# One stage for experts, overflow and the last norm of a hybrid decoder layer

## Chip, core and metric

The kernel is one program on one core of a Trainium2 chip. The metric is the device time of one execution in microseconds (us), and a kernel's time is the median of its runs. Everything is computed in float32.

## What is computed

One layer of a decoder trunk on 1024 real and 16 meta tokens of width 1024: a combined input projection, latent attention, a gated linear recurrence, a gated merge with an output projection, then a mixture of 64 experts, and a last RMS norm. The change touches only what follows the routing. The reference there, cut down:

```python
def hier_moe(xf, w_group, b_group, w_route, b_route, w1, w3, w2):
    g_logits = (xf @ w_group + b_group).astype(jnp.float32)
    ...
    gate = (p_sel * jax.nn.softmax(top_val, axis=-1)).astype(xf.dtype)
    expert = g_sel[:, None] * EXPERTS_PER_GROUP + top_idx        # two experts per token
    ...
    def expert_block(args):
        tok, e = args
        xb = x_pad[tok]
        hdn = jax.nn.silu(xb @ w1[e]) * (xb @ w3[e])
        return hdn @ w2[e]
    ...
# in reference():
        h = h + merged @ w_out[l]
        u = rmsnorm(h, ffn_norm[l])
        h = h + hier_moe(u.reshape(B * L, D), ...)
    return rmsnorm(h, final_norm)[:, N_META:]
```

Each of 1024 tokens goes to two of 64 experts. An expert has 3 MB of weights: w1 and w3 (1024 x 256 each) and w2 (256 x 1024).

## The kernel before

The program is a row of stages. Each is a block in which five engines have their own instruction streams and meet only at semaphores; at its end all engines drain, a barrier follows, the stage's semaphores are cleared, and a second barrier follows. Four stages matter here.

`phase_output` computes the residual `h` and the normed `u2`, stores both to memory, and routes: a table says which tokens each expert gets, 64 slots to an expert in the first pass. While it runs it also loads the weights of experts 0 to 2 (`AHEAD = 3`).

`phase_experts` works through the 64 experts in order. All engines run the same loop `each_expert`, whose iteration `e` holds work for several neighbouring experts:

- SyncE (SP) loads the weights of expert `e + 3` into buffer `(e + 3) % 4`, w1 and w3 (`load_up`) once the up product of expert `e - 1` has been made, w2 (`load_down`) once its down product has.
- GpSimd (POOL) gathers the 64 token rows of expert `e + 3` into `m_x` by an indirect DMA (L1908), and scatters the result of expert `e - 2` from `m_y` to `y_moe` by another (L1915), in this order.
- TensorE (PE) makes the up product of `e` (L1992, 32 matmuls), turns the rows of `e + 1` (L2001), makes the down product of `e - 1` (L2010), and turns `m_hid` of `e` (L2016).
- ScalarE (ACT) makes the sigmoid of `e`, copies the turned rows of `e + 1`, and copies the down product of `e - 1`, scaled, into `m_y`.
- VectorE (DVE) copies the row numbers for the gather of `e + 3` (`m_src_row`, L1962), those for the scatter of `e` (`m_dst_row`, L1967), makes `m_prod` and `m_hid` of `e` (L1969, L1971), and copies the turned `m_hid` (`m_hT`, L1973).

There are `NBUF = 4` buffers of the weights, of `m_x`, of `m_y` and of both kinds of row numbers. A buffer of row numbers for the scatter is used again when the scatter that read it has landed, so VectorE waits in iteration `e` for the scatter of `e - 4`:

```python
                if inside(e):
                    if inside(e, -NBUF):
                        dve.wait_ge(y_out[b], 16 * n)
                        settle(dve, g)
                    dve.tensor_copy(dst_row[b][:, :], rows[:, 0, bass.ds(e, 1)]).then_inc(dst_ok, 1)
                    dve.wait_ge(sig_ok, e + 1)
```

`phase_overflow` does the experts that have more than 64 tokens; each engine reads the largest count and branches (L2045). In the profile nothing of its loop runs. `phase_final` walks 8 tiles of 128 tokens: SP loads `z_h` (512 KB) and the two expert results of each token `z_y` (1 MB) four tiles ahead; VectorE adds both (L2227), ScalarE squares, sums and takes the root (L2214, L2216), VectorE inverts (L2230) and multiplies (L2233), and GpSimd issues the store (L2204). `z_y` can't be loaded before the last scatter has landed, and the whole of `phase_final` starts behind it.

Of the kernel before, what the change touches and what calls it, by code (L numbers as in the profile page):

```python
# [48 lines left out]
NBUF = 4  # L49
AHEAD = 3  # L50
SKIP = 4096.0
# [1771 lines left out]

def inside(e, d=0):

    return not isinstance(e, int) or 0 <= e + d < EXPERTS


def each_expert(eng, body):

    for e in range(-3, NBUF):
        body(e, e // NBUF, e % NBUF)
    with eng.Fori(1, EXPERTS // NBUF - 1) as n:
        for b in range(NBUF):
            body(NBUF * n + b, n, b)
    for e in range(EXPERTS - NBUF, EXPERTS + 3):
        body(e, e // NBUF, e % NBUF)


def turn(n, b, d):  # L1840


    return n + (b + d) // NBUF, (b + d) % NBUF


def phase_experts(nc, g):

    HALF = DE // 2
    with ExitStack() as ph:
# [7 lines left out]
        y = [sb(f"m_y{b}", [CAP, D]) for b in range(NBUF)]  # L1862
# [7 lines left out]
        y_out = [sem(f"m_y_out{b}") for b in range(NBUF)]  # L1870
# [8 lines left out]
        @block.sync
        def _(sp):  # L1880
            for c in range(2):
                sp.dma_start(tab[:, c * CAP * ROWS:(c + 1) * CAP * ROWS],
                             g.table.rearrange("(e s) r -> e s r", e=EXPERTS)[:, 0:CAP, :]
                             .rearrange("e s r -> e (s r)")).then_inc(tab_in, 16)

            def body(e, n, b):
                if inside(e, 3) and (not isinstance(e, int) or e >= AHEAD - 3):
                    wait(sp, up_mm, e)
                    g.load_up(sp, e + 3, turn(n, b, 3)[1])
                    wait(sp, dn_mm, e)  # L1890
                    g.load_down(sp, e + 3, turn(n, b, 3)[1])

            each_expert(sp, body)

        @block.gpsimd
        def _(pool):
            for b in range(NBUF):
                pool.memset(x[b][:, :], 0.0).then_inc(x_zero, 1)
            pool.wait_ge(x_zero, NBUF)

            def body(e, n, b):
                if inside(e, 3):
                    xb = turn(n, b, 3)[1]
                    pool.wait_ge(src_ok, e + 4)
                    settle(pool, g)
                    wait(pool, x_tr, e)
                    settle(pool, g)
                    pool.indirect_dma_start(out=x[xb][:, :], out_offset=None, in_=g.u2,  # L1908
                                            in_offset=bass.IndirectOffsetOnAxis(ap=src_row[xb][:, 0:1], axis=0),
                                            bounds_check=SEQ - 1, oob_is_err=False).then_inc(x_in[xb], 16)  # L1910
                if inside(e, -2):
                    yb = turn(n, b, -2)[1]
                    pool.wait_ge(y_ok, 2 * e - 2)
                    settle(pool, g)
                    pool.indirect_dma_start(out=g.y, out_offset=bass.IndirectOffsetOnAxis(ap=dst_row[yb][:, 0:1], axis=0),  # L1915
                                            in_=y[yb][:, :], in_offset=None,
                                            bounds_check=2 * SEQ - 1, oob_is_err=False).then_inc(y_out[yb], 16)

            each_expert(pool, body)
            for b in range(NBUF):  # L1920
                pool.wait_ge(y_out[b], 16 * (EXPERTS // NBUF))

        @block.scalar
        def _(act):
            def body(e, n, b):
                if inside(e):
                    act.wait_ge(up_mm, e + 1)
                    act.activation(sig[b % 2][:, :], bank(UP_BANK + b % 2, 0, HALF), ACT.Sigmoid).then_inc(sig_ok, 1)  # L1928
                if inside(e, 1):
                    act.wait_ge(x_tr, e + 2)  # L1930
                    act.activation(xT[(b + 1) % 2][:, :, :],
                                   bank(X_BANK + (b + 1) % 2).rearrange("p (j t) -> p j t", j=DK), ACT.Copy).then_inc(xT_ok, 1)
                if inside(e, -1):
# [12 lines left out]
            each_expert(act, body)

        @block.vector
        def _(dve):
            dve.wait_ge(tab_tr, 1)  # L1950
            dve.tensor_copy(rows[:, 0, :], bank(H_BANK + 1, 0, EXPERTS, 0, CAP)).then_inc(rows_ok, 1)
            dve.tensor_copy(gate[:, :], bank(H_BANK + 1, EXPERTS, EXPERTS)).then_inc(rows_ok, 1)
            dve.tensor_copy(rows[:, 1, :], bank(H_BANK + 1, 2 * EXPERTS, EXPERTS, 0, CAP)).then_inc(rows_ok, 1)
            dve.wait_ge(rows_ok, 3)

            def body(e, n, b):
                if inside(e, 3):
                    sn, s = turn(n, b, 3)
                    if inside(e, 3 - NBUF):
                        dve.wait_ge(x_in[s], 16 * sn)  # L1960
                        settle(dve, g)
                    dve.tensor_copy(src_row[s][:, :], rows[:, 1, bass.ds(e + 3, 1)]).then_inc(src_ok, 1)  # L1962
                if inside(e):
                    if inside(e, -NBUF):
                        dve.wait_ge(y_out[b], 16 * n)
                        settle(dve, g)
# [366 lines left out]
```

## Time and profile before

| | us |
|---|---|
| median of 3 runs | 1761.7 (1757.5 to 1764.3) |
| the profiled execution | 1760.33 |
| its span | 1758.6 |
| granted clock of TensorE over the span | 0.92 |

The span counts from the first to the last instruction of the program; the 1.7 us beside it are launch and return. The page cuts the span into 40 slices of 44 us:

```profile
PE   4999999999985979888797987497888888788810
...
DMA  5111111222120310000574851499999999999736
GB/s 145 48 35 36 28 36 61 84 92 91 58 51 16 78 32 1 1 1 1 171 243 146 318 169 72 138 382 391 398 392 395 393 395 395 391 388 383 301 142 263
```

The experts run from about 1111 us to 1695 us (slices 26 to 38), a third of the span, with the DMA engines full; overflow and last norm are the rest.

### The profile page before, as it was taken

To read this page: it belongs to the slowest core of one execution; us is meant where nothing else is said; L and a number is where in the kernel's file an instruction comes from. 1 tells how busy PE (TensorE), PEld (TensorE's weight loads), DVE (VectorE), ACT (ScalarE), POOL (GpSimd) and SP (SyncE) were. 2 spreads that over 40 slices of the span, in tenths; PEclk is the share of its full clock that TensorE was granted. 3 is DMA by queue.
4 is the path that set the end of the run, shared out by engine and by line. 5 is a ranking of instruction groups with operands and counts; after the bars stand their busy time and mean duration, and the time that the engine had idled before them with its cause. 6 is when DMAs were issued, how large, how long until landed. Compare 5 with 4: busy or idle time off the path is not lost. (4 is left out here: it accounts for less than half of the span.)

```text
span 1758.6 us, 23922 instructions
## 1 busy us (share of the span) xinstructions
PE 1430.1 (81%) x8664; PEld 1028.2 (58%) x8664; DVE 637.4 (36%) x1525; ACT 545.7 (31%) x1011; POOL 158.0 (9%) x201
## 2 busy tenths in 40 slices
PE   4999999999985979888797987497888888788810
PEld 4888887788775756555585876254444444444400
DVE  4455654311028654666453367111111111111115
ACT  5534433222122334455310343132222222222212
POOL 0000000000000000000000011222222112222100
PEclk8999999999988997999898988699999999999965
DMA  5111111222120310000574851499999999999736
GB/s 145 48 35 36 28 36 61 84 92 91 58 51 16 78 32 1 1 1 1 171 243 146 318 169 72 138 382 391 398 392 395 393 395 395 391 388 383 301 142 263
DMA packets 132583, 314.91 MB, mean 179 GB/s; under 512 B 24400, under 2 KB 80848, under 8 KB 115104
## 3 DMA queue, kind: packets, MB, share of 16 engines
q1 hardware_dynamic: 118304, 284.53, 44.7%
q0 software_dynamic: 14208, 29.42, 4.8%
q8 instruction: 46, 0.75, 0.2%
q14 instruction: 25, 0.20, 0.0%
HBM read 284.45 MB, written 43.02 MB: 186 GB/s over the span
## 5 line engine op out<-in xcount | busy, mean ns | idle before, releaser
L1992 PE MATMUL ps<-r,m_xT 128*64 128x256 f32 x2048 | 262.0, 414 | 89.5 <-DMA r<-in_w 88.2
L1992 PEld LDWEIGHTS ps<-r,m_xT 128*64 128x64 f32 x2048 | 158.8, 149 | 175.3 <-issue 115.7
L129 PE MATMUL ps<-uTh,h_wh 128*128 128x512 f32 (+2 forms) x608 | 234.9, 386 | 7.9 <-DVE uTl L424 7.1
L130 PE MATMUL ps<-uTl,h_wh 128*128 128x512 f32 (+2 forms) x608 | 227.4, 374 | 0.0
L131 PE MATMUL ps<-uTh,h_wl 128*128 128x512 f32 (+2 forms) x608 | 227.1, 373 | 0.0
L1969 DVE TENSOR_TENSOR m_prod<-m_sig,ps 128x128 f32<-128x128 f32 x64 | 18.4, 287 | 337.3 <-ACT m_sig L1928 337.3
L129 PEld LDWEIGHTS ps<-uTh,h_wh 128*128 128x128 f32 x608 | 115.4, 190 | 29.8 <-DVE uTl L424 7.7
L131 PEld LDWEIGHTS ps<-uTh,h_wl 128*128 128x128 f32 x608 | 115.4, 190 | 18.3
L130 PEld LDWEIGHTS ps<-uTl,h_wh 128*128 128x128 f32 x608 | 115.8, 190 | 17.0
L2010 PE MATMUL ps<-r,m_hT 128*64 128x512 f32 x512 | 123.9, 605 | 0.4 <-issue 0.4
L1941 ACT ACTIVATE m_y<-ps,m_gate 64x512 f32<-64x512 f32 x128 | 87.5, 683 | 98.7 <-PE ps L2010 97.1
L1928 ACT ACTIVATE m_sig<-ps 128x128 f32<-128x128 f32 x64 | 17.8, 278 | 263.5 <-PE ps L1992 263.5
L1908 POOL DMA_INDIRECT m_x<-u_moe,m_src_row x64 | 59.9, 937 | 401.0 <-ACT m_y L1941 287.4
L429 DVE TENSOR_TENSOR h_wl<-h_w,h_wh 128x1024 fp32r<-128x1024 f32 x34 | 41.5, 1222 | 115.4 <-ACT h_wh L291 115.4
L2001 PEld LDWEIGHTS ps<-ident,m_x 64*128 64x128 f32 x512 | 61.2, 200 | 34.3 <-issue 34.3
L2001 PE MATMUL ps<-ident,m_x 64*128 64x64 f32 x512 | 70.0, 277 | 9.8 <-DMA m_x<-u_moe,m_src_row 9.8
L1286 PE MATMUL ps<-KT,QT 96*128 96x512 f32 (+3 forms) x192 | 74.9, 501 | 0.0
L1297 PE MATMUL ps<-ident,t_p 128*128 128x128 f32 (+1 forms) x288 | 46.3, 289 | 32.1 <-DVE t_p L1231 30.4
L1973 DVE COPY m_hT<-ps 128x128 f32<-128x128 f32 x64 | 18.7, 292 | 139.7 <-PE ps L2016 139.7
L1164 ACT ACTIVATE t_p<-ps,t_negmax 112x128 f32<-112x128 f32 (+7 forms) x64 | 47.3, 740 | 60.4 <-DVE t_negmax L1223 60.3
L486 DVE SCALAR_TENSOR_TENSOR h_S<-h_S,h_dec,ps 128x128 f32<-128x128 f32 x124 | 43.0, 347 | 57.5 <-PE ps L644 47.6
L1915 POOL DMA_INDIRECT y_moe<-m_y,m_dst_row x64 | 59.4, 928 | 46.6 <-ACT m_y L1941 26.9
(321 smaller groups left out, 2244.5 us busy)
## 6 DMA issues: line engine op xcount, KB each, us to landing
r<-in_w SPq DMA_DIRECT2D x192, 1024.0 KB, 21.9
h_w<-in_w_in SPq DMA_DIRECT2D x34, 512.0 KB, 4.2
e_gate<-gates SPq DMA_DIRECT2D x16, 512.0 KB, 5.4
z_y<-y_moe SPq DMA_DIRECT2D x8, 1024.0 KB, 8.9
gates<-h_f POOLq DMA_DIRECT2D x8, 512.0 KB, 2.9
gates<-h_b POOLq DMA_DIRECT2D x8, 512.0 KB, 2.9
e_wo<-in_w_out SPq DMA_DIRECT2D x4, 1024.0 KB, 10.0
merged<-e_m SPq DMA_DIRECT2D x8, 512.0 KB, 3.0
```

The source lines that it names most:

```text
L129: pe.matmul(out, lh, rh, start=start, stop=False)
L130: pe.matmul(out, lh, rl, start=False, stop=False)
L131: return pe.matmul(out, ll, rh, start=False, stop=stop)
L1164: act.activation(pr[b][0:rows(i), 0:P * (i + 1)], score(b, i, 0, P * (i + 1)), ACT.Exp, bias=negmax[0:rows(i), b:b + 1], accum_out=total[0 ...
L1286: ins = pe.matmul(score(b, i, c, w), g.QT[:, h, qcol(i):qcol(i) + rows(i)], g.KT[:, h, c:c + w], start=True, stop=True)
L1297: ins = pe.transpose(g.ps[:, (T_BANK + tbank(i, b, gi)) * 512 + x * P: (T_BANK + tbank(i, b, gi)) * 512 + x * P + rows(i)], pr[b][0:rows(i ...
L1908: pool.indirect_dma_start(out=x[xb][:, :], out_offset=None, in_=g.u2, in_offset=bass.IndirectOffsetOnAxis(ap=src_row[xb][:, 0:1], axis=0), ...
L1915: pool.indirect_dma_start(out=g.y, out_offset=bass.IndirectOffsetOnAxis(ap=dst_row[yb][:, 0:1], axis=0), in_=y[yb][:, :], in_offset=None, ...
L1941: act.activation(y[yb][:, q * 512:(q + 1) * 512], bank(Y_BANK + (b + 1) % 2, 0, 512, CAP * q, CAP * (q + 1)), ACT.Copy, scale=gate[CAP * q ...
L1992: ins = pe.matmul(bank(UP_BANK + b % 2, 0, DE, CAP * h, CAP * (h + 1)).rearrange("p (r f) -> p r f", r=2), xT[b % 2][:, j, :], g.r13[b][:, ...
L2001: ins = pe.transpose(bank(X_BANK + xb % 2, j * CAP, CAP), x[xb][:, j::DK], g.ident[0:CAP, 0:CAP])
L2010: ins = pe.matmul(bank(Y_BANK + db % 2, 0, 512, CAP * h, CAP * (h + 1)), hT[:, j, :], g.r2[db][:, j, 512 * h:512 * (h + 1)], start=j == 0, ...
```

## The change

`phase_experts`, `phase_overflow` and `phase_final` become one stage `phase_moe`.

- Weights, `m_x` and `m_src_row` get five buffers (`NBUF = 5`); weights are loaded four experts ahead (`LOOK = 4`), of which three still come from `phase_output`. `m_y` and `m_dst_row` get two buffers (`YB = 2`).
- The loop has ten experts in its body and runs four times; 10 experts ahead of it and 14 behind it are written out. Before, the body had four.
- At its head SP loads `z_h` (8 x 512 KB) and the gain (512 KB) behind the weights of experts 3 and 4.
- The overflow uses buffers of the expert part and semaphores of its own.
- In the last norm SP loads `z_y` into the weight buffers of experts (`pair`), all 8 at once, when GpSimd says that every scatter has landed (`all_out`); GpSimd adds the first result to `z_h`, VectorE the second; VectorE adds tile `t` before it inverts and multiplies tile `t - 1`; SP issues the stores.

```diff
-NBUF = 4
+NBUF = 5
 AHEAD = 3
+LOOK = NBUF - 1
...
+    YB = 2
...
-        y = [sb(f"m_y{b}", [CAP, D]) for b in range(NBUF)]
+        y = [sb(f"m_y{b}", [CAP, D]) for b in range(YB)]
...
-        dst_row = [sb(f"m_dst_row{b}", [CAP, 1], I32) for b in range(NBUF)]
+        dst_row = [sb(f"m_dst_row{b}", [CAP, 1], I32) for b in range(YB)]
...
+                if isinstance(e, int) and e == 0:
+                    for t in range(TT):
+                        sp.dma_start(h[:, t, :], g.h[t * P:(t + 1) * P, :]).then_inc(h_in, 16)
+                    sp.dma_start(gain[:, :], g.final_norm[None, :].to_broadcast([P, D])).then_inc(gain_in, 16)
...
+            sp.wait_ge(all_out, 1)
+            for t in range(TT):
+                sp.dma_start(pair[t], y_src[t * P:(t + 1) * P, :, :]).then_inc(pair_in[t], 16)
+            for t in range(TT):
+                sp.wait_ge(o_ok, t + 1)
+                sp.dma_start(g.out[0, t * P:(t + 1) * P, :], pair[t][:, 0, :]).then_inc(stored, 16)
...
+            late_blocks(pool, late)
+            pool.sem_inc(all_out, 1)
+            pool.wait_ge(h_in, 16 * TT)
+            for t in range(TT):
+                pool.wait_ge(pair_in[t], 16)
+                pool.tensor_tensor(h[:, t, :], h[:, t, :], pair[t][:, 0, :], ALU.add).then_inc(first_ok, 1)
...
                 if inside(e):
-                    if inside(e, -NBUF):
-                        dve.wait_ge(y_out[b], 16 * n)
+                    yn, yb = turn(n, b, 0, YB)
+                    if inside(e, -YB):
+                        dve.wait_ge(y_out[yb], 16 * yn)
                         settle(dve, g)
...
+            late_blocks(dve, late)
+            dve.wait_ge(gain_in, 16)
+            for t in range(TT + 1):
+                if t < TT:
+                    dve.wait_ge(first_ok, t + 1)
+                    dve.tensor_tensor(h[:, t, :], h[:, t, :], pair[t][:, 1, :], ALU.add).then_inc(sum_ok, 1)
+                if t:
+                    dve.wait_ge(rt_ok, t)
+                    dve.reciprocal(st[:, 1, t - 1:t], st[:, 1, t - 1:t]).then_inc(rc_ok, 1)
...
```

What this moves on the engines, at three places. VectorE in the expert stage, iterations 2 and 3, before (`m_src_row` is the gather's, `m_dst_row` the scatter's; names behind "waits" are semaphores under the name that their number had first):

```order
1003 L1962 COPY m_src_row1<-m_rows 64x1 [waits h_ul_ok]
1004 L1967 COPY m_dst_row2<-m_rows 64x1
1005 L1969 TENSOR_TENSOR m_prod<-m_sig0,ps 128x128 [waits h_lf_ok]
1006 L1971 TENSOR_TENSOR m_hid<-m_prod,ps 128x128 [waits h_b_ok]
1007 L1973 COPY m_hT<-ps 128x128 [waits h_sig_q]
1008 L1962 COPY m_src_row2<-m_rows 64x1 [waits h_consts]
1009 L1967 COPY m_dst_row3<-m_rows 64x1
```

and in the changed kernel:

```order
1003 L2077 COPY m_src_row0<-m_rows 64x1 [waits h_consts]
1004 L2083 COPY m_dst_row0<-m_rows 64x1 [waits h_w_in1]
1005 L2085 TENSOR_TENSOR m_prod<-m_sig0,ps 128x128 [waits h_b_ok]
1006 L2087 TENSOR_TENSOR m_hid<-m_prod,ps 128x128 [waits h_vt_ok]
1007 L2089 COPY m_hT<-ps 128x128 [waits h_q_ok]
1008 L2077 COPY m_src_row1<-m_rows 64x1 [waits h_cst]
1009 L2083 COPY m_dst_row1<-m_rows 64x1 [waits h_wh_ok]
```

The order is the same, but `m_dst_row` has a wait from expert 2 on, which is for the scatter of two experts earlier (before, from expert 4 on, for that of four earlier). SP at the head of the expert stage, before:

```order
203 L1882 DMA m_tab<-slots 64x256 x2
204 L1370 DMA r13_3<-in_w1 128x2048
205 L1370 DMA r13_3<-in_w3 128x2048
206 L1374 DMA r2_3<-in_w2 128x2x1024
207 L1370 DMA r13_0<-in_w1 128x2048 [waits h_f_ok]
```

and in the changed kernel:

```order
203 L1926 DMA m_tab<-slots 64x256 x2
204 L1371 DMA r13_3<-in_w1 128x2048
205 L1371 DMA r13_3<-in_w3 128x2048
206 L1375 DMA r2_3<-in_w2 128x2x1024
207 L1371 DMA r13_4<-in_w1 128x2048
208 L1371 DMA r13_4<-in_w3 128x2048
209 L1375 DMA r2_4<-in_w2 128x2x1024
210 L1939 DMA z_h<-h_mid 128x1024 x8
211 L1940 DMA z_gain<-in_final_norm 128x1024
212 L1371 DMA r13_0<-in_w1 128x2048 [waits h_lf_ok]
```

The weights of expert 4, `z_h` and the gain need no wait there. GpSimd at the end of the changed kernel, behind the branches of the overflow:

```order
172 L2016 TENSOR_TENSOR z_h<-z_h,r_1 128x1024 [waits h_sg_out0,h_hi_ok]
173 L2016 TENSOR_TENSOR z_h<-z_h,r_1 128x1024 [waits h_sg_out1]
...
178 L2016 TENSOR_TENSOR z_h<-z_h,r_4 128x1024 [waits z_pair_in6]
179 L2016 TENSOR_TENSOR z_h<-z_h,r_4 128x1024 [waits z_pair_in7]
180 L1858 UNCONDITIONAL_BRANCH
181 L105 ISA [waits barrier_Pool_Activation_PE_DVE_SP_gather]
```

The eight adds stand between the last scatter and the stage's end, where GpSimd drains; before, the drain came right behind the last scatter.

## Rows read from the trace of the kernel before

**Rows 1.** Windows: us, busy us of each engine, granted TensorE clock, DMA share, GB/s

```profile
1130.00:1145.00 15.00, 14.52 (x110) 9.30 (x108) 1.96 (x10) 3.12 (x6) 2.38 (x3) 0.94 0.55 194
...
1200.00:1640.00 440.00, 360.65 (x2417) 202.38 (x2419) 54.89 (x245) 109.83 (x196) 92.74 (x100) 0.94 1.02 392
...
1700.00:1740.00 40.00, 0.00 (x0) 0.00 (x0) 21.49 (x22) 12.03 (x20) 2.77 (x5) 0.50 0.98 392
```

**Rows 2.** Waits from 1200 to 1640 us: total us, times, longest

```profile
PE ps L1992 <- DMA r<-in_w: 81.3, 50, 2.7
...
SPq L1374 <- PE ps L2010: 230.0, 49, 8.7
```

**Rows 3.** Timeline around expert 33: start, us, engine, line, operation [idle before <- releaser]

```profile
1403.54 0.33 PE L2016 MATMUL ps<-ident,m_hid 128*128 128x128 f32 x1
...
1404.23 0.15 DVE L1962 COPY m_src_row<-m_rows 64x1 int32 x1
...
1405.40 0.94 POOL L1908 DMA_INDIRECT m_x<-u_moe,m_src_row  x1 [5.10 <-ACT m_y L1941]
...
1405.92 3.67 PE L1992 MATMUL ps<-r,m_xT 128*64 128x256 f32 x32 [2.05 <-DMA r<-in_w]
1406.64 0.93 POOL L1915 DMA_INDIRECT y_moe<-m_y,m_dst_row  x1 [0.30 <-issue]
...
1409.95 0.29 DVE L1969 TENSOR_TENSOR m_prod<-m_sig,ps 128x128 f32<-128x128 f32 x1 [5.35 <-ACT m_sig L1928]
1410.27 0.29 DVE L1971 TENSOR_TENSOR m_hid<-m_prod,ps 128x128 f32<-128x128 f32 x1
...
1410.55 1.94 PE L2010 MATMUL ps<-r,m_hT 128*64 128x512 f32 x8
...
1412.41 0.33 PE L2016 MATMUL ps<-ident,m_hid 128*128 128x128 f32 x1
...
1415.26 5.25 PE L1992 MATMUL ps<-r,m_xT 128*64 128x256 f32 x32 [2.52 <-DMA r<-in_w]
```

**Rows 4.** DMA issues in 1406 to 1407 and 1678 to 1679 us: the scatter's us to landing

```profile
y_moe<-m_y,m_dst_row POOLq DMA_INDIRECT x1, 7.5
...
y_moe<-m_y,m_dst_row POOLq DMA_INDIRECT x1, 2.5
```

**Rows 5.** The scatters (ns, first and last start), and four turnings from the timeline

```profile
L1915 POOL DMA_INDIRECT y_moe<-m_y,m_dst_row x64: 901/929/932, 1144.5 to 1681.3; - x64
...
1197.72 0.33 PE L2016 MATMUL ps<-ident,m_hid 128*128 128x128 f32 x1
...
1645.08 0.33 PE L2016 MATMUL ps<-ident,m_hid 128*128 128x128 f32 x1
...
1651.96 0.33 PE L2016 MATMUL ps<-ident,m_hid 128*128 128x128 f32 x1
...
1676.14 0.33 PE L2016 MATMUL ps<-ident,m_hid 128*128 128x128 f32 x1
```

**Rows 6.** GpSimd's drain at the end of expert and last stage: ns, start

```profile
L1854 POOLq DRAIN  x1: 10517/10517/10517, 1684.6 to 1684.6; - x1
...
L2161 POOLq DRAIN  x1: 721/721/721, 1757.2 to 1757.2; - x1
```

**Rows 7.** Last stage, by tile: ns min/median/max, first and last start us; load of 1 MB; branch

```profile
L2227 DVE TENSOR_TENSOR z_h<-z_h,z_y x16: 1217/1224/1225, 1706.8 to 1749.0; 128x1024 f32<-128x1024 f32 x16
...
L2214 ACT ACTIVATE z_junk<-z_h x8: 1056/1056/1056, 1709.3 to 1750.3; 128x1024 f32<-128x1024 f32 x8
...
L2233 DVE SCALAR_TENSOR_TENSOR z_o<-z_h,z_stat,z_gain x8: 1283/1284/1285, 1712.3 to 1752.0; 128x1024 f32<-128x1024 f32 x8
...
z_y<-y_moe SPq DMA_DIRECT2D x1, 1024.0 KB, 5.6
...
L2045 POOLq TENSOR_LOAD <-most x1: 502/502/502, 1697.0 to 1697.0; - x1
```

**Rows 8.** GpSimd's groups, by form: busy us, mean ns

```profile
L1153 POOL TENSOR_SCALAR_AFFINE_SELECT t_mask<-t_mask 128x128 f32<-128x128 f32 x1 | 0.3, 289 | 0.2 <-POOL t_rest_q L1150 0.2
```

More of the change, by code:

```diff
@@ L1829, in each_expert, with turn, phase_moe @@
 def each_expert(eng, body):
[L1831 to L1846, printed above, removed]
+    rounds = (EXPERTS - PERIOD) // PERIOD
+    for e in range(-LOOK, PERIOD):
+        body(e, e // PERIOD, e % PERIOD)
+    with eng.Fori(1, rounds) as n:
+        for b in range(PERIOD):
+            body(PERIOD * n + b, n, b)
+    for e in range(PERIOD * rounds, EXPERTS + 3):
+        body(e, e // PERIOD, e % PERIOD)
+def turn(n, b, d, size):
+    return n * (PERIOD // size) + (b + d) // size, (b + d) % size
+def phase_moe(nc, g):
     HALF = DE // 2
+    LATE = (SLOTS // CAP - 1) * EXPERTS
+    YB = 2
     with ExitStack() as ph:
@@ L1875, in phase_experts @@
+        square = g.r2[1][:, 0, :]
+        h_in, gain_in, stored = sem("z_h_in"), sem("z_gain_in"), sem("z_stored")
+        pair_in = [sem(f"z_pair_in{t}") for t in range(TT)]
+        first_ok, sum_ok, ss_ok, rt_ok, rc_ok, o_ok = (sem("z_first_ok"), sem("z_sum_ok"), sem("z_ss_ok"), sem("z_rt_ok"),
+                                                       sem("z_rc_ok"), sem("z_o_ok"))
+        y_src = g.y.rearrange("(t c) d -> t c d", c=2)
         block = ph.enter_context(nc.Block())
         bank = lambda i, a=0, n=512, r0=0, r1=P: g.ps[r0:r1, i * 512 + a:i * 512 + a + n]
+        late_bank = lambda i, a=0, n=512, rows=P: g.ps[0:rows, i * 512 + a:i * 512 + a + n]
@@ L1877, in phase_experts @@
+        turned = lambda i, n: late_bank(i, 0, n * CAP).rearrange("p (j t) -> p j t", j=n)
         UP_BANK, X_BANK, Y_BANK, H_BANK = 0, 2, 4, 6
[L1879 to L1921, printed above, removed]
@@ L2085, in body, with late @@
+            each_expert(pool, body)
+            for b in range(YB):
+                pool.wait_ge(y_out[b], 16 * (EXPERTS // YB))
+            pool.sem_inc(v_turn, 1)
+            def late(k, e, c):
+                pool.wait_ge(v_rows_ok, k + 1)
                 settle(pool, g)
-                pool.indirect_dma_start(out=x[:, :], out_offset=None, in_=g.u2,
-                                        in_offset=bass.IndirectOffsetOnAxis(ap=rows[:, 2:3], axis=0),
-                                        bounds_check=SEQ - 1, oob_is_err=False).then_inc(x_in, 16)
@@ L2244, in program @@
+                        ins = pe.matmul(late_bank(Y_BANK + q, rows=CAP), late_hT[:, j, :],
+                                        g.r2[0][:, j, q * 512:(q + 1) * 512], start=j == 0, stop=j == 1)
+                    ins.then_inc(v_dn_mm, 1)
+            late_blocks(pe, late)
 def program(nc, a, out):
```

421 lines of the change are left out of this document (188 added, 233 removed).

## The prediction

> **What bounds the kernel now.** I read the page for the stages, then the windows, the waits, the timeline of a few experts and the landing times. The stages up to the routing are untouched, so only the time from 1111 us on counts. From 1200 to 1640 us the DMA engines are full (share 1.02, 392 GB/s) while TensorE is busy 361 of 440 us [rows 1]; TensorE's up product waits for weights, 81 us in 50 waits [rows 2]. One expert takes (1645.08 - 1197.72) / 50 = 8.95 us, read between experts 9 and 59 at the turning of m_hid [rows 5]. Where weights are there, TensorE needs only 1651.96 - 1645.08 = 6.9 us [rows 5]. So the middle is bound by transfers, with 2 us of slack per expert in everything else. Behind it come a tail with no weights left, GpSimd's drain of 10.5 us from 1684.6 us on [rows 6], two stage borders, and a last norm from the first add at 1706.8 us [rows 7] to the end at 1758.6 us, bound by its own chain: (1749.0 - 1706.8) / 7 is about 5.7 us per tile, of which VectorE works 2 x 1.22 + 1.28 and ScalarE's square 1.06 [rows 7].
>
> **The weights' fifth buffer and h at the head.** From 1130 to 1145 us the DMA share is 0.55 [rows 1], so about 7 us are idle there: four buffers are full and expert 0 has freed none yet. The added 4.5 MiB (4.7 MB) of h and gain take 4.7 / 0.392 = 12.0 us; they and expert 4 fill this gap. A net cost of 0 to 5 us remains on the weights' stream, if that stream is still the bound. Once the stream is full, a fifth buffer brings nothing: transfers at 392 GB/s don't care how far ahead they were asked for.
>
> **The two y buffers.** This is the step that I hold to decide. In iteration e VectorE may write m_dst_row only when the scatter of e - 2 has landed. Behind that wait on VectorE stand m_prod and m_hid of e, for which TensorE's turning waits, and behind it on TensorE all of the next expert. And the scatter of e - 2 is itself issued late: GpSimd issues the gather of e + 3 first, which waits for m_src_row in the same iteration. That closes a ring from one turning to the next [rows 3]:
> - turning at 1403.54, m_src_row (behind m_hT) at 1404.23, gather 1405.40, scatter 1406.64: 3.1 us;
> - landing of that scatter: 7.5 us with the queues full, 2.5 us with nothing else under way [rows 4];
> - then the copy of the row numbers (0.15, some 0.35 us with its semaphores by estimate), m_prod to the end of m_hid (1409.95 to 1410.56, 0.6 us) and 0.15 us to TensorE: 1.1 us.
>
> So the ring takes 4.2 us + the landing, 11.7 us with full queues, against 8.95 us. Before, the same wait reached back four experts, so it had two more rounds (18 us) for 7.5 us and never showed. The ring beats the transfers, the stock of weights loaded ahead grows until all buffers are full, and SP's queue then runs empty once per expert; in such a pause the scatter lands sooner. The pace settles between. Let it be C. SP issues one expert's 8.95 us of transfers when a down product ends, which is about 6.9 us behind a turning, so 3.8 us behind the scatter's issue; its data begin to flow about 1.3 us later (estimate: 5.6 us of a 1 MB load [rows 7] with 0.5 MB ahead of it, less 1.5 MiB / 392 GB/s = 4.0, leaves 1.6 for both ends). The previous expert's transfers thus last r = 8.95 - C + 3.8 + 1.3 beyond the scatter's issue, and the scatter lands some 1.5 us behind them. C = 4.2 + 1.5 + 14.05 - C gives **C = 9.9 us**. One more effect: behind an idle time of 2.05 us the up product took 3.67 us, behind one of 2.52 us it took 5.25 us [rows 3]; I read that as the clock granted at its lower level, 1.2 GHz, for a part (the mean grant from 1200 to 1640 us is 0.94 [rows 1]). At C = 9.9 TensorE stands still for 3 us in each round. That makes the down product, and so the next burst, 1.6 us later: r grows by 1.6 and C to 10.7 us. I take the middle, **10.3 us**. It can't be under 8.95 (the transfers) nor over 11.7 (the full landing time).
>
> **The sum of the expert stage.** First scatter at 1144.5 us [rows 5] as before, landing 7.5, 1.1 to the turning of expert 2: 1153.1. In the next four rounds the queues are still full, since h, gain and the experts 3 to 11 are 12 + 9 x 8.95 = 93 us of transfers from 1113 us on: 4 x 11.7 = 46.8, turning of expert 6 at 1199.9 us. Then 54 x 10.3 = 556.2: expert 60 at 1756.1. Behind the last load the landing is short and TensorE's 6.8 us rule: 3 x 6.8 = 20.4, expert 63 at 1776.5 us, where before it was 1676.14 [rows 5]. From there to the landing of the last scatter it is 1684.6 - 1676.1 = 8.5 us as before [rows 5, 6]: **1785.0 us**, against 1684.6.
>
> **Borders, drain and last norm.** Before, from 1684.6 to 1758.6 us: 74.0 us. After: GpSimd reads the count (0.5 us [rows 7]) and branches, and SP wakes: 1.3 us (between 0.5 and the 1.8 us from there to the first load before, a barrier included). First 1 MB: 4.7 us (the 5.6 us above with 0.5 MB ahead, the wait for its issue counted). Then eight adds of GpSimd. No row shows such an add. Lower end: it is hidden by the loads, 1 MiB at 392 GB/s = 2.67 us per tile. GpSimd's select over 128 columns took 0.289 us [rows 8]; eight times that is 2.3 us for 1024 columns, also hidden. Upper end: it takes turns with VectorE's add and product (1.22 + 1.28 [rows 7]) for the memory, 2.3 + 2.5 = 4.8 us. I take 3.5 us, midway, as VectorE works in 2.5 of every 2.7 us when the pipeline is full: 28 us. Then the drain: it took 10.5 us after 128 DMAs of GpSimd and 0.72 us after 8 [rows 6], 82 to 90 ns each, so it is a price per DMA that is paid at the drain, however long ago they ended. It now begins behind the last add. Beside it run VectorE's add 1.2, square and root 1.5, inversion and product 1.5, and store to the end 5.3 (1758.6 less 1752.0 + 1.28 [rows 7]), 9.5 us in all, so the drain is the later: 10.5 + 0.7 for the barriers. Sum: 1.3 + 4.7 + 28 + 11.2 = **45.2 us**, between 38.2 (adds hidden: 1.3 + 4.7 + 7 x 2.67 + 2.3 + 11.2) and 55.6 (4.8 us each). The gain is 74.0 - 45.2 = 28.8 us: the drain isn't saved, the borders and the serial chain of the tiles are.
>
> The Trainium skill has a rule against GpSimd's part ("GPSIMD Engine Reference", sections "Elementwise — side-by-side cycle accounting" and "Engine selection"): an add of two tensors belongs on VectorE, since GpSimd took 4497 ns for 2048 columns where VectorE took 2293, and the two share an interface to the memory. The estimate from that page is 2.25 us per tile, by which the last norm alone would give the 38.2 us end; its word on the shared interface would give the 55.6 us end. No row here shows either.
>
> **Total.** 1785.0 + 45.2 = 1830.2 us of span, + 1.7 = **1832 us**, against 1760.33 of the profiled run, which lies 1.4 us under the median of 1761.7.
>
> **Rivals.**
> - *The wait doesn't hold.* VectorE finds the scatter landed in time, and weights remain the bound: last landing at 1684.6 as before, + 45.2 + 1.7 = 1731.5 us, up to 5 more for h. This is the other side, faster. It decides by the landing time: under 8.95 - 4.2 = 4.75 us the ring is hidden. For it: unloaded it is 2.5 us. Against it: it is 7.5 us whenever the weights' queue is full, and only with a full queue are the weights the bound. Chance 0.11.
> - *The ring holds only at the start, then the pace is that of the transfers*, 8.95 us: expert 60 at 1199.9 + 54 x 8.95 = 1683.2, last landing 1683.2 + 20.4 + 8.5 = 1712.1, + 46.9 = 1759 us. The stock of loaded weights is lost and that is about all of the gain. It needs the scatter to pass a full queue in 4.75 us. Chance 0.09.
> - *The landing never gets shorter*: 54 x 11.7 = 631.8, last landing 1860.6, + 46.9 = 1907 us. For it: a scatter issued at 3.8 us ahead of a burst may meet it each time. Chance 0.08.
> - *GpSimd's backlog of 128 DMAs is worked off before its first add* rather than at the drain: the adds begin 10.5 us later, the end is then VectorE's 9.5 us: some 9 us more, 1840 us. Chance 0.04.
>
> **How the numbers follow.** My forecast has 0.68: C from 9.9 to 10.7 moves it by 22 us down or up, the adds by 7 down and 10 up, so 1803 to 1864 us. About 0.5%, 9 us, is what a measurement of this kernel can tell from no change. Faster by more than that is the first rival, 0.11; within it the second, 0.09; slower all the rest, 0.80. The range leaves out the first and the third rival (0.19) and reaches from the second to the forecast's upper end: 1757 to 1866 us.
>
> **What would show it.** In the changed kernel VectorE's m_dst_row should end long waits whose releaser is the scatter's DMA, about 60 of them; the spacing of the turnings should be 11.7 us up to expert 6, 10.3 on average later (perhaps long and short by turns), 6.8 at the end; TensorE's wait for weights should be gone, the DMA share from 1200 to 1640 us should fall from 1.02 to about 0.87, and scatters should land in 4 to 7 us. GpSimd's drain of 10.5 us should stand at the very end; its add gives the price that I had to bound. Spacings of 8.95 us with TensorE waiting for weights would prove the central step wrong.

## The result and the profile after

The changed kernel takes 1839.9 us (median of 4 runs, 1838.2 to 1845.1) where the kernel before takes 1762.7 us: a ratio of 1.045, 95% interval 1.042 to 1.048. It is 77 us slower. 1832 us was forecast. The profiled execution has a span of 1836.4 us; all rows below are from its trace unless another kernel is named.

The windows of the expert stage and of the last norm, with the columns of [rows 1]:

```profile
1130.00:1145.00 15.00, 14.52 (x110) 8.97 (x106) 1.89 (x9) 3.99 (x8) 2.81 (x3) 1.00 1.04 398
1200.00:1640.00 440.00, 328.35 (x2024) 177.67 (x2022) 44.78 (x210) 93.27 (x166) 76.78 (x83) 0.85 0.85 323
...
1794.00:1820.00 26.00, 0.00 (x0) 0.00 (x0) 22.19 (x10) 7.06 (x13) 24.23 (x8) 0.50 0.80 330
1820.00:1832.00 12.00, 0.00 (x0) 0.00 (x0) 11.68 (x15) 5.78 (x12) 0.00 (x0) 0.50 0.46 183
```

From 1200 to 1640 us the DMA share has fallen from 1.02 to 0.85, the granted clock from 0.94 to 0.85, and TensorE is busy 328 us instead of 361 [rows 1]. Neither the transfers nor TensorE is the bound any more. The waits from 1200 to 1750 us (in total, times, longest) name what is:

```profile
DVE m_dst_row L2083 <- DMA y_moe<-m_y,m_dst_row: 459.2, 52, 10.9
...
PE ps L2154 <- DVE m_hid L2087: 138.6, 44, 5.7
```

The wait for weights (81.3 us in 50 waits in [rows 2]) isn't in that list. On the page, the groups of the up product, of VectorE's copy and of the turning (busy, mean ns, idle before and its releaser) say the same:

```profile
L2130 PE MATMUL ps<-r,m_xT 128*64 128x256 f32 x2048 | 299.0, 457 | 1.9 <-ACT m_xT L2026 1.2
...
L2083 DVE COPY m_dst_row<-m_rows 64x1 int32 (+1 forms) x64 | 9.3, 146 | 533.4 <-DMA y_moe<-m_y,m_dst_row 533.4
L2154 PE MATMUL ps<-ident,m_hid 128*128 128x128 f32 x64 | 23.2, 362 | 156.9 <-DVE m_hid L2087 156.8
```

VectorE's copy costs 146 ns and stands behind 533 us of waiting for scatters. Most of that is harmless. What counts is the 157 us in which TensorE then waits for `m_hid`.

The timeline of two rounds shows the ring, as [rows 3] showed its parts before:

```profile
1398.53 0.45 PE L2154 MATMUL ps<-ident,m_hid 128*128 128x128 f32 x1 [4.74 <-DVE m_hid L2087]
...
1398.91 5.60 PE L2130 MATMUL ps<-r,m_xT 128*64 128x256 f32 x32
...
1399.24 0.15 DVE L2077 COPY m_src_row<-m_rows 64x1 int32 x1
...
1401.60 0.93 POOL L1988 DMA_INDIRECT y_moe<-m_y,m_dst_row  x1 [0.31 <-issue]
...
1407.45 0.38 SPq L1375 DMA_DIRECT2D r<-in_w  x1
...
1407.90 0.15 DVE L2083 COPY m_dst_row<-m_rows 64x1 int32 x1 [8.52 <-DMA y_moe<-m_y,m_dst_row]
...
1408.77 0.30 PE L2154 MATMUL ps<-ident,m_hid 128*128 128x128 f32 x1 [1.36 <-DVE m_hid L2087]
...
1409.00 3.67 PE L2130 MATMUL ps<-r,m_xT 128*64 128x256 f32 x32
...
1411.78 0.93 POOL L1988 DMA_INDIRECT y_moe<-m_y,m_dst_row  x1 [0.30 <-issue]
...
1415.60 0.38 SPq L1375 DMA_DIRECT2D r<-in_w  x1
...
1418.76 0.14 DVE L2083 COPY m_dst_row<-m_rows 64x1 int32 x1 [9.19 <-DMA y_moe<-m_y,m_dst_row]
...
1419.62 0.30 PE L2154 MATMUL ps<-ident,m_hid 128*128 128x128 f32 x1 [4.06 <-DVE m_hid L2087]
```

Turning to scatter takes 3.07 and 3.01 us (forecast 3.1), the scatter to VectorE's copy 6.30 and 6.98 us, the copy to the next turning 0.87 us (forecast 1.1 with the semaphore's way). The turnings at four experts, to be set beside [rows 5]:

```profile
1150.76 0.45 PE L2154 MATMUL ps<-ident,m_hid 128*128 128x128 f32 x1 [5.27 <-DVE m_hid L2087]
...
1194.11 0.30 PE L2154 MATMUL ps<-ident,m_hid 128*128 128x128 f32 x1 [1.32 <-DVE m_hid L2087]
...
1752.83 0.30 PE L2154 MATMUL ps<-ident,m_hid 128*128 128x128 f32 x1 [0.20 <-DVE m_hid L2087]
...
1780.88 0.30 PE L2154 MATMUL ps<-ident,m_hid 128*128 128x128 f32 x1 [0.92 <-DVE m_hid L2087]
```

These are experts 2, 6, 59 and 63. From 6 to 59 a round takes 558.7 / 53 = 10.54 us, from 59 to 63 7.0 us.

### The profile page after: what moved, and what is told of

Read it like the earlier page. It is cut to its first block and busy times, and to the rows that moved or that the text cites. A ratio compares the mean times of both kernels' runs of the same rounds, so it can differ in the third digit from the quotient of the medians.

```text
span 1836.4 us, 23386 instructions
## 1 busy us (share of the span) xinstructions
PE 1471.7 (80%) x8664; PEld 1041.7 (57%) x8664; DVE 637.1 (35%) x1517; ACT 541.8 (30%) x1008; POOL 178.2 (10%) x201
## 5 line engine op out<-in xcount | busy, mean ns | idle before, releaser
L2130 PE MATMUL ps<-r,m_xT 128*64 128x256 f32 x2048 | 299.0, 457 | 1.9 <-ACT m_xT L2026 1.2
L2130 PEld LDWEIGHTS ps<-r,m_xT 128*64 128x64 f32 x2048 | 171.7, 166 | 111.0 <-issue 63.1
L2083 DVE COPY m_dst_row<-m_rows 64x1 int32 (+1 forms) x64 | 9.3, 146 | 533.4 <-DMA y_moe<-m_y,m_dst_row 533.4
L2154 PE MATMUL ps<-ident,m_hid 128*128 128x128 f32 x64 | 23.2, 362 | 156.9 <-DVE m_hid L2087 156.8
L2154 PEld LDWEIGHTS ps<-ident,m_hid 128*128 128x128 f32 x64 | 9.9, 155 | 210.2 <-issue 210.2
L430 DVE TENSOR_TENSOR h_wl<-h_w,h_wh 128x1024 fp32r<-128x1024 f32 x34 | 41.6, 1222 | 115.4 <-ACT h_wh L292 115.4
L1165 ACT ACTIVATE t_p<-ps,t_negmax 112x128 f32<-112x128 f32 (+7 forms) x64 | 47.3, 740 | 60.5 <-DVE t_negmax L1224 60.3
```

What stands on the lines that cost most here:

```text
L1165: act.activation(pr[b][0:rows(i), 0:P * (i + 1)], score(b, i, 0, P * (i + 1)), ACT.Exp, bias=negmax[0:rows(i), b:b + 1], accum_out=total[0 ...
L2130: ins = pe.matmul(bank(UP_BANK + b % 2, 0, DE, CAP * f, CAP * (f + 1)).rearrange("p (r f) -> p r f", r=2), xT[b % 2][:, j, :], g.r13[ub][: ...
```

## The experiments

Times are medians; "H2 to H63" is the time between the turnings of experts 2 and 63 in the trace, "norm" the time from the landing of the last scatter to the end of the span. These two don't move with where the stage happens to begin (up to 10 us apart between executions). The edits of y5, dst10 and swap are shown against the changed kernel, that of b_y2 against the kernel before, that of wait3 against dst10, and those of nb4, htail, vec and apart against y5.

| kernel | us | ratio to before [95%] | H2 to H63 | norm |
|---|---|---|---|---|
| before | 1762 | 1 | 527.8 | 74.3 |
| changed | 1839.9 | 1.045 [1.042, 1.048] | 630.1 | 47.3 |
| b_y2 | 1870.2 | 1.063 [1.060, 1.065] | 631.7 | 74.2 |
| swap | 1799.8 | 1.017 [1.011, 1.024] | 587.4 | 47.3 |
| y5 | 1739.0 | 0.987 [0.986, 0.989] | 532.9 | 47.5 |
| dst10 | 1737.1 | 0.986 [0.984, 0.988] | 532.7 | 47.2 |
| wait3 | 1736.5 | 0.987 [0.985, 0.988] | 529.9 | 47.3 |
| nb4 | 1733.5 | 0.984 [0.982, 0.987] | 528.6 | 48.1 |
| vec | 1730.9 | 0.983 [0.981, 0.985] | 532.2 | 41.3 |
| htail | 1728.7 | 0.982 [0.980, 0.984] | 520.9 | 47.5 |
| apart | 1744.1 (one run) | | 532.6 | 52.3 |
| best4 | 1732.9 | 0.983 [0.981, 0.985] | 527.8 | 41.6 |
| best | 1724.0 | 0.979 [0.977, 0.981] | 521.8 | 41.3 |

### Five y buffers in the changed kernel (y5)

```diff
-    YB = 2
+    YB = 5
...
```

To make room, the three intermediates of the overflow share one buffer, and the last waits for the scatters count as many as each buffer has had.

> The changed kernel with five buffers of m_y and m_dst_row instead of two (the overflow's three intermediates share one buffer to make room). VectorE then waits in iteration e for the scatter of e - 5. Theory (the ring through the landing of the scatter sets the pace): the ring has three more rounds of slack, the waits of m_dst_row vanish, TensorE waits for weights again, spacing of the turnings 8.95 us as in the kernel before, last scatter landed at 1684 to 1690 us, last norm 47 us as measured in the changed kernel, so 1731 to 1739 us in all, 101 to 109 us less than the changed kernel. Rival (something else in the one long stage, such as the ten-fold loop body, the fifth weight buffer or h at the head, slows the rounds): the time stays within 20 us of the changed kernel's 1840 us.

1739.0 us: the two buffers cost 101 us, more than the whole rest of the change gains. From 1200 to 1640 us TensorE's wait for weights is back, as in [rows 2], and no wait of `m_dst_row` is left:

```profile
PE ps L2131 <- DMA r<-in_w: 83.1, 47, 2.9
```

### Ten buffers of the row numbers, two of y (dst10)

```diff
-        dst_row = [sb(f"m_dst_row{b}", [CAP, 1], I32) for b in range(YB)]
+        dst_row = [sb(f"m_dst_row{b}", [CAP, 1], I32) for b in range(PERIOD)]
...
-                    if inside(e, -YB):
-                        dve.wait_ge(y_out[yb], 16 * yn)
+                    if inside(e, -PERIOD):
+                        dve.wait_ge(y_out[yb], 16 * (yn - PERIOD // YB + 1))
...
```

VectorE's copy and GpSimd's scatter take the buffer that belongs to the expert, `dst_row[b]`; `PERIOD` is 10.

> The changed kernel with ten buffers of m_dst_row, so that VectorE waits for the scatter of e - 10; m_y keeps its two buffers, so that ScalarE still waits in iteration e for the scatter of e - 3 before it writes y of e - 1. Theory (it is VectorE's early wait, with m_prod and m_hid behind it, that closes the ring): ScalarE's wait reaches one round further back and has only the copy of the down product behind it, so the rounds are near 8.95 us again and the time is that of the kernel with five buffers of both, 1731 to 1745 us. Rival (it is the number of m_y buffers, whoever waits): near the changed kernel, 1820 to 1840 us.

1737.1 us. `m_y` is 4 KB per partition and `m_dst_row` 4 bytes; the whole loss hangs on the 4 bytes. ScalarE's wait for the scatter of e - 3, which `m_y` needs, costs nothing that these times can show.

### The same, with a wait for the scatter of e - 3 (wait3)

```diff
-                    if inside(e, -PERIOD):
-                        dve.wait_ge(y_out[yb], 16 * (yn - PERIOD // YB + 1))
+                    if inside(e, -3):
+                        wn, wb = turn(n, b, -3, YB)
+                        dve.wait_ge(y_out[wb], 16 * (wn + 1))
```

> The changed kernel with ten buffers of m_dst_row (1737.1 us with a wait for the scatter of e - 10), but VectorE waits in iteration e for the scatter of e - 3: one expert further back than in the changed kernel, and seven nearer than its buffers need. Nothing else differs, so this varies the reach of the wait alone. Theory (a ring of 4.2 us + the landing of 7.5 us now has two rounds instead of one): 11.7 us against 2 x 8.95 = 17.9 us, the ring is hidden, the wait of m_dst_row vanishes, 1735 to 1741 us. Rival (the cost falls off slowly with the reach, since anything that VectorE waits for in a round holds TensorE up now and then): 10 to 50 us over 1737 us.

1736.5 us, the same as dst10. The waits from 1200 to 1640 us in this kernel:

```profile
PE ps L2132 <- DMA r<-in_w: 82.9, 48, 3.0
...
DVE m_dst_row L2085 <- DMA y_moe<-m_y,m_dst_row: 59.7, 37, 3.3
```

The theory had the time right and one detail wrong: the wait doesn't vanish. VectorE still waits 60 us in 37 waits, and nobody is late for it, since TensorE is waiting for weights meanwhile. So the cost steps with the reach of the wait: 101 us at e - 2, nothing at e - 3.

### The kernel before with two y buffers (b_y2)

```diff
-        y = [sb(f"m_y{b}", [CAP, D]) for b in range(NBUF)]
+        y = [sb(f"m_y{b}", [CAP, D]) for b in range(2)]
...
-        dst_row = [sb(f"m_dst_row{b}", [CAP, 1], I32) for b in range(NBUF)]
+        dst_row = [sb(f"m_dst_row{b}", [CAP, 1], I32) for b in range(2)]
...
```

The waits follow: VectorE waits for the scatter of e - 2, ScalarE for that of e - 3.

> The kernel before with m_y and m_dst_row cut from four buffers to two, and nothing else. Theory: this part alone carries the loss of the expert stage, rounds of 10.3 to 10.6 us instead of 8.95, so 54 to 60 rounds x 1.35 to 1.65 us = 75 to 98 us over the kernel before, about 1835 to 1860 us. With four weight buffers the stock of loaded weights is one expert smaller, which matters to neither as the ring is the bound. Rival (the two buffers hurt only together with the rest of the change): within 20 us of the kernel before.

1870.2 us, 108 us over the kernel before, and H2 to H63 is that of the changed kernel within 2 us. This part alone makes the slow rounds. The expectation was 10 us too low for a reason of arithmetic: it multiplied 54 to 60 rounds by the difference to 8.95 us, but the first rounds of the kernel before live on loaded weights and take 6.8 us each (expert 2 at 1148.3, expert 6 at 1175.4 us), where here they take 10.4. Expert 2 itself, the first that waits for a scatter, turns 4.8 us later than before (1153.1 us).

### GpSimd's scatter ahead of its gather (swap)

```diff
+                if inside(e, -2):
+                    yb = turn(n, b, -2, YB)[1]
+                    pool.wait_ge(y_ok, 2 * e - 2)
...
                 if inside(e, 3):
                     xb = turn(n, b, 3, NBUF)[1]
...
-                if inside(e, -2):
```

> The changed kernel with GpSimd's two DMAs of an iteration in the other order: first the scatter of e - 2, then the gather of e + 3. The scatter no longer waits behind the gather's issue (1.2 us) nor for m_src_row. Theory (the scatter lands behind the weights that are under way, so an earlier issue waits longer for them): the landing gets longer by most of what the issue gains, the pace stays at 10.2 to 10.6 us and the time within 25 us of 1840 us. Rival (the landing takes a fixed time after issue): the ring is 1.2 to 2 us shorter per round, 54 x 1.2 = 65 us or more are gained, 1735 to 1775 us.

1799.8 us: 40 us less, and neither theory expected it (one allowed 25, the other asked for 65). One of its four executions took only 1777.4 us, which stays unexplained; the trace is of one at 1801.6 us. The landing did get longer, as the theory has it: from the scatter to VectorE's copy it is 7.3 us on average (6.5 to 8.1) at an average round of 9.8 us, where the changed kernel has mostly 7 to 8.7 us in one round and 4.1 to 6.3 in the next, 6.6 on average. What I had misjudged is the other thing that the order changes. The gather waits for `m_src_row`, which stands on VectorE behind the turning. With the scatter first, the scatter needs only the copied `m_y`, that is a down product which ends ahead of the turning. I had priced this as 1 to 2 us off the same ring, but it makes another ring. The timeline of the kernel with the exchanged order:

```profile
1348.65 0.93 POOL L1979 DMA_INDIRECT y_moe<-m_y,m_dst_row  x1 [9.66 <-ACT m_y L2036]
...
1355.67 0.15 DVE L2083 COPY m_dst_row<-m_rows 64x1 int32 x1 [8.92 <-DMA y_moe<-m_y,m_dst_row]
...
1356.53 0.45 PE L2154 MATMUL ps<-ident,m_hid 128*128 128x128 f32 x1 [3.79 <-DVE m_hid L2087]
...
1356.91 4.89 PE L2130 MATMUL ps<-r,m_xT 128*64 128x256 f32 x32
...
1364.62 0.33 PE L2154 MATMUL ps<-ident,m_hid 128*128 128x128 f32 x1
...
1367.27 0.93 POOL L1979 DMA_INDIRECT y_moe<-m_y,m_dst_row  x1 [7.98 <-ACT m_y L2036]
```

The ring now goes over two rounds: scatter to copy 7.0, to the turning 0.9, a whole round of TensorE with a slow up product 8.1, to the next scatter 2.6, together 18.6 us here, and 2 x 9.8 on average. It is longer than 2 x 8.95 = 17.9, so it still binds, but only just: TensorE waits for `m_hid` in every other round.

### Four weight buffers (nb4), and h behind the last weights (htail)

```diff
-NBUF = 5
+NBUF = 4
...
-    YB = 5
+    YB = 4
```

> The kernel with five buffers of m_y and m_dst_row (1739.0 us), but with four buffers of the weights, of m_x, m_src_row, m_y and m_dst_row, weights loaded three experts ahead as before. It differs from the kernel before by the joined stage, h at the head and the last norm. Theory (a fifth weight buffer brings nothing once the stream is full, and h and the gain fill the gap at the head as well as expert 4's weights do): 1736 to 1743 us, the same as 1739.0 within 0.3%. At the head the 12 us of h and gain meet a gap of 7 us here too, so up to 5 us may be added. Rival (the fifth buffer carries a part of the gain of joined kernels): 8 us or more over 1739.0 us, since 3 MB of weights, 8 us of transfers, can't be asked for before the first buffer is free.

```diff
-                if isinstance(e, int) and e == 0:
-                    for t in range(TT):
-                        sp.dma_start(h[:, t, :], ...).then_inc(h_in, 16)
-                    sp.dma_start(gain[:, :], ...).then_inc(gain_in, 16)
...
+            for t in range(TT):
+                sp.dma_start(h[:, t, :], ...).then_inc(h_in, 16)
+            sp.dma_start(gain[:, :], ...).then_inc(gain_in, 16)
```

The added lines stand behind the loop over the experts.

> The kernel with five buffers of m_y and m_dst_row (1739.0 us), but h and the gain are loaded behind the last weights instead of at the head. Theory (at the head they fill a gap of 7 us with 12 us of transfers, the rest delays all weights): 0 to 5 us less, 1734 to 1739 us; the last weights come up to 5 us earlier, and h has the 20 us of the last rounds to arrive. Rival (at the tail the 12 us of transfers stand ahead of the last scatters and the first results' load): up to 4 us more, the last scatters landing in 7 us instead of 3.

nb4 took 1733.5 us, 5.5 less than y5, and htail 1728.7 us, 10.3 less; both are below what was expected. With `NBUF = 4` the loop's body also has 8 experts instead of 10, since `PERIOD` is twice `NBUF`. The windows from 1113 to 1150 us, where the experts begin, of the kernel before, nb4, y5 and htail in this order:

```profile
1113.00:1150.00 37.00, 23.67 (x164) 14.83 (x166) 3.80 (x23) 7.24 (x12) 8.88 (x10) 0.75 0.67 228
```

```profile
1113.00:1150.00 37.00, 24.39 (x164) 15.23 (x166) 3.80 (x23) 7.23 (x12) 9.77 (x11) 0.74 0.98 358
```

```profile
1113.00:1150.00 37.00, 23.32 (x166) 14.69 (x168) 3.80 (x23) 7.23 (x12) 11.28 (x13) 0.76 0.95 343
```

```profile
1113.00:1150.00 37.00, 24.84 (x166) 15.49 (x168) 3.80 (x23) 7.23 (x12) 10.41 (x12) 0.74 0.90 324
```

Before, the DMA share of 0.67 leaves 0.33 x 37 = 12.2 us idle at the head, not the 7 us that I had read from 15 us of it. With four buffers h and the gain (12.0 us) fit: H2 to H63 grows by 0.8 us only. With five and h, 20 us of transfers are to fill 12: + 5.1 us. With five and h at the tail the 8 us of expert 4 fit and H2 to H63 is 6.9 us shorter. The step from y5 to htail is 532.9 - 520.9 = 12.0 us, exactly the transfers of h and the gain. At the tail they cost 1.8 us: the last scatter landed in 4.9 us instead of 3.1. What stays open is some 3 us between nb4 (528.6) and y5 (532.9): 0.03 x 37 = 1.1 us more idle time at the head is in the rows, and the rest is larger than the spread among the kernels with the expert loop of y5 and h at its head (y5, vec and apart, 532.2 to 532.9). The shorter loop body of nb4 was not tried by itself.

### The last norm: GpSimd's adds by themselves (apart), and without them (vec)

```diff
             dve.wait_ge(gain_in, 16)
+            dve.wait_ge(first_ok, TT)
```

> The kernel with five buffers of m_y and m_dst_row, but VectorE starts the last norm only when GpSimd has made all eight adds. It measures GpSimd's add by itself. Theory (the two engines slow each other at the memory): GpSimd's add takes 2.3 us in place of 3.06, and VectorE's add and product, which then run alone, 1.2 and 1.3 us each in place of 3.3 and 3.2; GpSimd's drain begins behind its last add and ends 10.5 us later, beside VectorE's 8 tiles. Total 5.6 + 8 x 2.7 (the loads' pace) + 8 x 2.53 + 6 = 53 to 55 us from the last scatter's landing, 1744 to 1748 us. Rival (the 3.06 us are GpSimd's own price and the slow VectorE has another cause): the adds stay at 3.06 us and VectorE's operations are as slow as before.

```diff
-            pool.wait_ge(h_in, 16 * TT)
-            for t in range(TT):
-                pool.wait_ge(pair_in[t], 16)
-                pool.tensor_tensor(h[:, t, :], h[:, t, :], pair[t][:, 0, :], ALU.add).then_inc(first_ok, 1)
...
+                    dve.wait_ge(pair_in[t], 16)
+                    dve.tensor_tensor(h[:, t, :], h[:, t, :], pair[t][:, 0, :], ALU.add).then_inc(first_ok, 1)
```

> The kernel with five buffers of m_y and m_dst_row (1739.0 us; 47.5 us from the last scatter's landing to the end), but VectorE makes both adds of the last norm and GpSimd none, so GpSimd drains as soon as it has said that the scatters have landed. Theory (beside GpSimd's adds VectorE's add and product take 3.2 to 3.4 us instead of 1.2 to 1.3; alone it is faster with three operations per tile than with two beside GpSimd): 5.6 us to the first tile, 8 x (1.22 + 1.22 + 1.28) = 30 us, 5.3 us for the last product's store to the end, plus 1 to 2 us: 42 to 44 us, so 1733 to 1736 us. The 10.5 us of GpSimd's drain lie under the loads. Rival (GpSimd's adds take work off VectorE and help): 8 x 1.22 = 10 us longer, 1745 to 1750 us.

First the changed kernel's adds and products (min/median/max ns, first and last start), then the adds of GpSimd and VectorE in the kernel that keeps them apart:

```profile
L2016 POOL TENSOR_TENSOR z_h<-z_h,r x8: 2338/3318/3322, 1795.3 to 1816.4; 128x1024 f32<-128x1024 f32 x8
...
L2106 DVE TENSOR_TENSOR z_h<-z_h,r x8: 1211/2288/3407, 1797.7 to 1828.3; 128x1024 f32<-128x1024 f32 x8
...
L2111 DVE SCALAR_TENSOR_TENSOR r<-z_h,z_stat,z_gain x8: 1285/1286/3176, 1804.5 to 1831.3; 128x1024 f32<-128x1024 f32 x8
```

```profile
L2017 POOL TENSOR_TENSOR z_h<-z_h,r x8: 2337/2337/2337, 1696.5 to 1713.8; 128x1024 f32<-128x1024 f32 x8
...
L2108 DVE TENSOR_TENSOR z_h<-z_h,r x8: 1216/1218/1225, 1716.2 to 1734.3; 128x1024 f32<-128x1024 f32 x8
```

Alone, a GpSimd add takes 2.34 us and a VectorE add 1.22. Together they take 3.32 and 3.35, and VectorE's product 3.17 instead of 1.28. While GpSimd adds two tiles (6.6 us), VectorE gets through one add and one product (6.5 us). Taking strict turns would make 2 x 2.34 + 1.22 + 1.28 = 7.2 us, no contention 4.7. So they nearly take turns. The ScalarE square stays at 1.06 us. The loads of `z_y` are not what slows the two: from 1696 to 1716 us of apart the DMA share is 0.86 while GpSimd's adds take 2.34 us, and from 1690 to 1706 us of vec it is 1.02 while VectorE's take 1.22. The Trainium skill ("GPSIMD Engine Reference", section "Specifications") says that GpSimd shares its SBUF interfaces with VectorE and that instructions of VectorE with two SBUF inputs contend for them. The trace agrees: the add and the product, with two such inputs each, took 3.35 and 3.17 us.

VectorE alone is quicker: 41.3 us instead of 47.5 (vec), and the median is 8.1 us less, of which 6.2 are seen in the last norm. Both vec and, from the landing to the end, apart (52.3 us) came out slightly under what was expected. GpSimd's drain (ns, start) in vec, in apart and in the changed kernel:

```profile
L1858 POOLq DRAIN  x1: 10517/10517/10517, 1685.7 to 1685.7; - x1
```

```profile
L1858 POOLq DRAIN  x1: 12921/12921/12921, 1713.8 to 1713.8; - x1
```

```profile
L1858 POOLq DRAIN  x1: 16239/16239/16239, 1814.0 to 1814.0; - x1
```

GpSimd's queue runs ahead of its last adds, so the drain begins before they end. It ends 10.5 to 10.6 us behind them: 1726.7 - 1716.1 in apart (last add 1713.8 + 2.34), 1830.2 - 1819.7 in the changed kernel (eight adds, 24.46 us from 1795.25). In vec, with no add, it is 10517 ns to the nanosecond as in [rows 6], and over 29 us ahead of the end. That the price goes by the number of DMAs was read from two drains (128 and 8 DMAs). The kernel before has a third that bears it out, at the end of `phase_output`, where GpSimd has issued 16:

```profile
L1534 POOLq DRAIN  x1: 1366/1366/1366, 1109.4 to 1109.4; - x1
```

From 8 to 16 DMAs it is 81 ns for each more, from 16 to 128 it is 82.

### Joining what helped (best, best4)

> Three edits together: five buffers of m_y and m_dst_row, both adds of the last norm on VectorE, h and the gain loaded behind the last weights. Theory (the three don't touch): 1739.0 us less 10.3 us (h at the tail, measured 1728.7) less 6.1 us (last norm 41.4 instead of 47.5 us in the traces) = 1722.6 us, 1720 to 1726 us. Rival (VectorE's adds now wait for h, which comes late, or its loads delay the first results): at most one of the two gains, 1727 to 1731 us.

> The same three edits, with four buffers of the weights, m_x, m_src_row, m_y and m_dst_row instead of five. Theory (the fifth buffer's only worth is that expert 4's 3 MB fill 8 us of the DMA engines' idle time at the head; in the traces from expert 2 to expert 63 it took 527.8 us with four buffers and no h, 528.6 with four and h, 532.9 with five and h, 520.9 with five and h at the tail): without h at the head four buffers take 527.8 us again, 7 us more than the kernel with five, 1728 to 1732 us. Rival (four buffers are as good, or 5 us better, as they were with h at the head: 1733.5 against 1739.0 us): 1717 to 1724 us.

best is y5 with the edits of htail and vec: 1724.0 us, 37 us under the kernel before, ratio 0.979, and 116 us under the changed kernel. The gains nearly add: 16.4 us were expected under y5 (10.3 of htail, and the 6.1 of vec that its trace shows in the last norm; by the medians it would be 18.4), 15.0 came. best4, with four buffers of each, takes 1732.9 us, 9 us more, of which H2 to H63 shows 6.0; in the two profiled executions the expert stage also began 4.9 us apart, which isn't the buffer's doing. So the fifth buffer of the weights is worth 6 to 9 us where h isn't at the head, and less than nothing where it is (nb4).

## Why the prediction was right, step by step

- **The ring decides.** Right, and shown: removing it (y5, dst10, wait3) gives 101 to 103 us, adding it to the kernel before (b_y2) costs 108. That VectorE's wait closes it, not ScalarE's, is shown by dst10.
- **4.2 us + the landing.** The fixed part is 3.0 us up to the scatter and 0.9 from the copy's start, together 3.9 us. swap, which takes the gather's issue and `m_src_row` out of the ring and shortens the rounds, bears out that both were in it.
- **First rounds, 11.7 us each.** Too long. The queues were full, yet the rounds from expert 2 to 6 took 43.35 / 4 = 10.8 us: from the scatter to VectorE's copy it was 5.9 to 8.1 us, 7.0 on average, not 7.5 each time. Expert 6 turned at 1194.1 instead of 1199.9 us; 2.9 us of that is the earlier start of the stage in this execution (expert 0 at 1131.5, before at 1134.4).
- **The pace of 10.3 us** measured 10.5: (1760.8 - 1194.1) / 54 = 10.49 up to expert 60. The two branches, 9.9 with a quick up product and 10.7 with a slow one, don't mix into a steady middle: over most of the stage rounds of 11 to 12.5 and of 8.4 to 10.4 us alternate. That the middle of the two branches was nearly met is in part luck, and "nor over 11.7 (the full landing time)" doesn't hold for single rounds, in which scatter to copy takes up to 8.7 us. The slow up product (over 4.5 us, in 32 of 64 rounds, before in 16) mostly follows a TensorE that stood still for over 4 us (5.60 us behind 4.74), the quick one (3.67) a short wait; around expert 47 there are also slow ones of 5.36 us behind waits of 1.9 to 2.5. Behind the slow one SP issues the next weights 5.9 us after the scatter (1401.60 to 1407.45), behind the quick one 3.8 us (1411.78 to 1415.60). That it is this shift which makes the next landing long was reasoned, not tried apart.
- **End of the expert stage.** Experts 60 to 63 took 20.1 us (forecast 20.4), expert 63 to the last landing 8.2 (8.5). The last scatter landed at 1789.1 instead of 1785.0 us: this 4.1 us is the pace's + 10.5 less the earlier expert 6's 5.8, and small things.
- **The last norm, 45.2 us** measured 47.3, but its working failed in one step. The first add begins 6.1 us after the landing (forecast 6.0) and the eight adds take 24.5 us (forecast 28, 3.06 each instead of 3.5). What comes behind them was put at 11.2 us, the drain, with VectorE needing only 9.5 us beside it. It was 16.7 us and VectorE's. The step that failed is "3.5 us per tile, since the two take turns": I charged the turns to GpSimd alone. VectorE was slowed 2.6-fold too and had five products left when GpSimd ended. The chain that ended last shows it:

```profile
1795.25 2.35 POOL z_h L2016
...
1797.70 6.69 DVE z_h L2106 x2
...
1807.67 3.28 DVE z_h L2106
...
1811.06 3.17 DVE r L2111
...
1820.80 1.13 DVE z_h L2106
...
1831.26 1.28 DVE r L2111
```

- **The drain is a price paid at the drain, however late.** Right, shown by vec and apart. It didn't set the end: it was over at 1830.2 us, 1 us before the last product.
- **h and the fifth buffer.** The net cost, 0 to 5 us, measured 5.1 for h, gain and expert 4 together (y5 against before, 532.9 - 527.8). "A fifth buffer brings nothing" is true in the full stream (391 GB/s from 1200 to 1640 us in y5, 392 before), but the head idles 12 us, not 7, and there it is worth 6 to 9 us (best against best4). The error was to take one window of 15 us for the whole gap.
- **The rivals.** The pace of 8.95 us with a lost stock, the full landing time each round, and the wait that doesn't hold are all out by the spacings; the last is what y5 made true, at 1739 us, where it was put at 1731.5 to 1736.5. The backlog that is worked off ahead of the first add is out too, since that add began 6.1 us after the landing.
- **The total.** The span came out 6.2 us over the forecast (1836.4 against 1830.2), which flatters the working: behind it stand -5.8 us up to expert 6, +10.5 from the pace, -3.5 from GpSimd's adds and +5.5 behind them. The mechanism was right, the nearness of the sum is partly luck.

## What to carry to other kernels

Before a buffer is made shallower, write down the ring that its release closes: from the release through every instruction that stands behind the wait on the same engine, back to the DMA that releases it, with that DMA's latency in a full queue. Divide by the number of rounds that the depth allows and compare with the pace; two rounds were enough here and one was not, and a small operand such as a row of indices can carry the ring while its large neighbour doesn't. A load that is moved should go where the DMA engines idle, read over the whole gap, and an elementwise operation moved to GpSimd should be priced with what it does to VectorE.

## What the runs showed of the hardware

- Side by side on 128 x 1024 float32 in SBUF, GpSimd's add went from 2.34 to 3.32 us and VectorE's from 1.22 to 3.35, its product from 1.28 to 3.17. VectorE suffered more. ScalarE's square (1.06 us) was untouched.
- GpSimd's drain took 10.5 us behind 128 indirect DMAs although they had all landed, and ended just as long behind eight adds (18.7 us of work in apart) where they stood between. Behind 16 DMAs it took 1.37 us, behind 8 it took 0.72.
- An indirect scatter of 64 rows landed in 7.0 us (swap) and 7.5 us (y5) at the median with the weights' queue full, 6.5 to 8.1 us in single cases; in 4.9 us beside the 512 KB loads at the tail (htail); and in 2.5 to 3.1 us with nothing else under way.
